# A hybrid decoder step on one core: one loop written out, the first norm reordered, the tail's parts in another order

## The reference

```
merged = sigmoid(ga) * u_a + sigmoid(gb) * u_b ;  mix = merged @ w_o
h = layer_norm(ALPHA * x + mix, ln1_w, ln1_b)
u = h @ w_up ;  g = h @ w_gate
acc = conv_b + sum_i up[:, i:i + t] * conv_w[i]       # up = the two earlier rows, then u
f = (gelu(acc) * g) @ w_down
y = layer_norm(ALPHA * h + f, ln2_w, ln2_b)
```

## Time and profile before

| | us |
|---|---|
| median of 3 runs | 2138.0 (2134.36 to 2139.96) |
| the profiled execution | 2139.22 |
| its span | 2137.5 |
| PE busy | 1989.5 (93%) |
| DVE busy | 1159.1 (54%) |
| ACT busy | 648.8 (30%) |
| POOL busy | 218.8 (10%) |

### The profile page before, as it was taken

The page is one execution under the profiler, slowest core; times in us unless marked ns, Lnnn a source line. Parts: engine busy times, 40 slices in busy tenths (PEclk is TensorE's granted clock), DMA queues, the critical chain, the costliest instruction groups (busy, mean ns, idle before and its releaser), DMA issues.

```text
span 2137.5 us, 39105 instructions
## 1 busy us (share of the span) xinstructions
PE 1989.5 (93%) x14335; PEld 1861.5 (87%) x14335; DVE 1159.1 (54%) x1771; ACT 648.8 (30%) x1179; POOL 218.8 (10%) x253
## 2 busy tenths in 40 slices
PE   7898998899999899989898898799999999999996
PEld 5796896798898798878798897799999999999996
DVE  4554454977867867885424856533322333233348
ACT  4444343134133223213401103434301322132224
POOL 1000000020020020020000101300000000100004
PEclk9999999999999999989999999899999999999999
DMA  4211101787987878886732310111111111111144
GB/s 126 63 32 50 40 21 51 233 311 245 310 281 262 301 264 298 278 308 231 252 94 89 106 49 11 40 49 40 50 49 50 40 48 43 54 42 49 43 142 131
DMA packets 151682, 276.50 MB, mean 129 GB/s; under 512 B 19042, under 2 KB 57951, under 8 KB 151543
## 3 DMA queue, kind: packets, MB, share of 16 engines
q1 hardware_dynamic: 115970, 175.26, 24.4%
q0 software_dynamic: 23232, 82.80, 13.0%
q10 hardware_dynamic: 12368, 16.88, 2.1%
HBM read 247.24 MB, written 27.72 MB: 129 GB/s over the span
## 4 chain that ended last, share of the span: by engine, by line
PE 44%; DVE 5%; DMA 1%; issue 1%; ACT 1%; SPq 0%; DVEq 0%; ACTq 0%
PE bank L121 40%; PE bank L1670 3%; DVE x_lo L1898 1%; DMA gated_raw<-gated_t_scratch 1%; DVE chunk_tmp L1827 1%; DVE chunk_tmp L1829 0%; DVE z L1895 0%; DVE moving_lo L1833 0%; DVE merged_hi L1831 0%; PE banks L1628 0%; DVE w_lo L1968 0%; DMA tail_raw<-in_w_down_dram 0%; DVE y L1944 0%; DMA z<-fox_t_scratch 0%; PE banks L1656 0%
## 5 line engine op out<-in xcount | busy, mean ns | idle before, releaser
L121 PE MATMUL bank<-x_hi,w_hi 128*128 128x344 f32 (+1 forms) x1944 | 641.5, 330 | 44.4 <-DVE x_lo L1898 15.1
L121 PE MATMUL bank<-x_lo,w_hi 128*128 128x344 f32 (+1 forms) x1944 | 631.6, 325 | 0.0
L121 PE MATMUL bank<-x_hi,w_lo 128*128 128x344 f32 (+1 forms) x1944 | 631.3, 325 | 0.0
L121 PEld LDWEIGHTS bank<-x_hi,w_hi 128*128 128x128 f32 (+1 forms) x1944 | 372.4, 192 | 61.6 <-issue 48.6
L121 PEld LDWEIGHTS bank<-x_lo,w_hi 128*128 128x128 f32 (+1 forms) x1944 | 372.5, 192 | 1.6
L121 PEld LDWEIGHTS bank<-x_hi,w_lo 128*128 128x128 f32 (+1 forms) x1944 | 372.1, 191 | 1.7
L97 ACT ACTIVATE w_hi<-w_raw 128x1024 fp32r<-128x1024 f32 (+3 forms) x139 | 142.1, 1022 | 453.7 <-PE bank L121 419.5
L121 PE MATMUL bank<-moving_hi,w_hi 128*128 128x344 f32 x744 | 227.0, 327 | 13.7 <-DVE moving_hi L1806 7.0
L121 PE MATMUL bank<-moving_lo,w_hi 128*128 128x344 f32 x744 | 237.6, 319 | 0.0
L104 DVE TENSOR_TENSOR w_lo<-w_raw,w_hi 128x1024 fp32r<-128x1024 f32 (+3 forms) x139 | 164.4, 1182 | 103.2 <-ACT w_hi L97 101.4
L121 PE MATMUL bank<-moving_hi,w_lo 128*128 128x344 f32 x648 | 208.1, 321 | 0.0
(11 more groups left out here) (275 smaller groups left out, 2781.3 us busy)
## 6 DMA issues: line engine op xcount, KB each, us to landing
cache_keys<-in_cache_k_dram SPq DMA_DIRECT2D x256, 256.0 KB, 4.8
cache_vals<-in_cache_v_dram SPq DMA_DIRECT2D x256, 256.0 KB, 5.1
w_raw<-in_w_in_dram POOLq DMA_DIRECT2D x52, 512.0 KB, 6.3
w_raw<-in_w_up_dram POOLq DMA_DIRECT2D x22, 512.0 KB, 4.5
w_raw<-in_w_gate_dram POOLq DMA_DIRECT2D x22, 512.0 KB, 4.5
tail_raw<-in_w_down_dram SPq DMA_DIRECT2D x22, 448.0 KB, 3.9
gate<-gate_t_scratch SPq DMA_DIRECT2D x15, 516.0 KB, 3.5
w_raw<-in_w_down_dram POOLq DMA_DIRECT2D x10, 448.0 KB, 4.4
```

What stands on the lines that cost most here:

```text
L121: mm = pe.matmul(g.bank[n][0:m, 0:TC], w[slot][:, k, 0:m], x[:, k, chunk(n)], start=(k == 0 and i == 0), stop=(k == kt - 1 and i == 2))
```

## The change

Three places. In `fox`, the loop of two rounds is written out on all five engines, so the waits are against constants and no branch is left.

In the first norm, the remaining order is: DVE splits the first gate job between the first and the second centring; then per chunk DVE only multiplies by rstd (`scale`), ACT applies weight and bias in place (`h_full`) and rounds in a second instruction, and DVE takes the remainder (`h_low`), alternating with the `scale` of the next chunk. PE works on up and gate of the first tile at once, chunk by chunk, slice by slice, the gate in three other banks. POOL takes its share of `acc` later, from the finished h. The first feed-forward tile is written out ahead of the loop on each engine, without the split that was moved.

In the tail, the parts are blocks 5 to 8, 2 to 4, and 0 and 1 (392, 384 and 256 columns), so seven blocks are spread over the tiles and two follow the last one. The second norm's weight and bias are issued behind four of the tail's weight tiles.

```diff
             def _(pe):
-                with pe.Fori(0, NIT) as it:
+                for it in range(NIT):
...
-    THIRD = 3
-    EDGE = (0, 3 * P, 6 * P, T)
-    tail = [(i, i // KD, i % KD) for i in range(NCH * KD)]
-    turned_after = {KD * (t // THIRD + 1) + 1 + 2 * (t % THIRD): t for t in range(2 * THIRD)}
+    PARTS = ((5, 6, 7, 8), (2, 3, 4), (0, 1))
+    SPANS = ((5 * P, T), (2 * P, 5 * P), (0, 2 * P))
+    ROWS = sum(PARTS, ())
+    EARLY = NT - len(PARTS[-1])
+    tail = [(i, i // KD, i % KD) for i in range(len(PARTS) * KD)]
+    part_of = [p for p, rows in enumerate(PARTS) for _ in rows]
+    turned_after = {KD * (part_of[r] + 1) + 1 + 2 * PARTS[part_of[r]].index(ROWS[r]): r for r in range(EARLY)}
...
-                for w, name in enumerate(("ln2_w", "ln2_b")):
-                    sp.dma_start(wide[w][:], a[name].to_broadcast([P, D])).then_inc(ln_land, 16)
                 for i, _, m in tail[RING:]:
+                    if i == RING + LANDS:
+                        for w, name in enumerate(("ln2_w", "ln2_b")):
+                            sp.dma_start(wide[w][:], a[name].to_broadcast([P, D])).then_inc(ln_land, 16)
...
                         up_and_gate(0, f0, ju)
+                        up_and_gate(1, f0, ju)
                         for k in range(NCH):
-                            pool.wait_ge(normed, (k + 1) * KD)
+                            pool.wait_ge(h_full, (k + 1) * KD)
+                            pool.wait_ge(h_lo, (k + 1) * KD)
                             for t in range(KD):
-                                ins = pool.tensor_scalar(acc[:, t, chunk(k)], z[:, t, chunk(k)], ln_cols[:, 1, t:t + 1], ALPHA, ALU.add, ALU.mult)
+                                ins = pool.tensor_scalar(acc[:, t, chunk(k)], z[:, t, chunk(k)], ALPHA, None, ALU.mult)
...
+                for n in range(NCH):
+                    for (j, slot), dst in ((up_job, bank[n]), (gate_job, gate_bank[n])):
+                        pe.wait_ge(g.w_split, RING + j + 1)
+                        pe.wait_ge(g.bank_free[n], ju + 1)
+                        for k in range(KD):
+                            pe.wait_ge(h_lo, n * KD + k + 1)
+                            for q, (w, x) in enumerate(((g.w_hi, g.xh), (g.w_hi, g.xl), (g.w_lo, g.xh))):
+                                mm = pe.matmul(dst[:, 0:TC], w[slot][:, k, :], x[:, k, chunk(n)],
+                                               start=(k == 0 and q == 0), stop=(k == KD - 1 and q == 2))
+                        mm.then_inc(g.mm_chunk, 1)
...
                         act.wait_ge(normed, n * KD + k + 1)
-                        act.activation(g.xh[:, k, chunk(n)], z[:, k, chunk(n)], ACT.Identity, bias=ln_cols[:, 1, k:k + 1]).then_inc(h_hi, 1)
+                        act.activation(z[:, k, chunk(n)], z[:, k, chunk(n)], ACT.Identity, scale=ln_cols[:, 0, k:k + 1], bias=ln_cols[:, 1, k:k + 1]).then_inc(h_full, 1)
+                        act.wait_ge(h_full, n * KD + k + 1)
+                        act.activation(g.xh[:, k, chunk(n)], z[:, k, chunk(n)], ACT.Copy).then_inc(h_hi, 1)
...
                 squares(0)
+                split_hi(g, act, job(JF, JF % 2, 1))
                 squares(1, range(0, 3))
...
+                centre(0)
+                split_lo(g, dve, job(JF, JF % 2, 1))
+                centre(1)
+                centre(2)
...
+                invert(0)
+                for k in range(KD):
+                    scale(0, k)
+                for n in range(NCH):
+                    if n < NCH - 1:
+                        invert(n + 1)
+                    for k in range(KD):
+                        h_low(n, k)
+                        if n < NCH - 1:
+                            scale(n + 1, k)
```

More of the change, by code:

```diff
@@ L424, in _ @@
             def _(pool):
-                with pool.Fori(0, NIT) as it:
+                for it in range(NIT):
                     for u in range(2):
@@ L438, in _ @@
                     sp.dma_start(dst[:], c[src]).then_inc(const_land, 16)
-                with sp.Fori(0, NIT) as it:
+                for it in range(NIT):
                     for u in range(2):
@@ L542, in _ @@
                 act.nop().then_inc(fo_out, 2)
-                with act.Fori(0, NIT) as it:
+                for it in range(NIT):
                     for u in range(2):
@@ L626, in _ @@
                 dve.wait_ge(const_land, 48)
-                with dve.Fori(0, NIT) as it:
+                for it in range(NIT):
                     for u in range(2):
@@ L1674, in _ @@
                         turn_rows(turned_after[i])
-                for t in range(2 * THIRD, NT):
-                    turn_rows(t)
+                for r in range(EARLY, NT):
+                    turn_rows(r)
             @block.scalar
@@ L1732, in _, with tile @@
                 h_high(2)
-                act.wait_ge(h_lo, NCH * KD)
                 act.wait_ge(z_part, 2)
                 for s, (f0, n, ju, jd) in enumerate(sections):
-                    with act.Fori(0, n) as i:
+                    def tile(i, first):
                         f = i + f0
-                        split_hi(g, act, job(i * 2 + ju, ju % 2, 1))
+                        if not first:
+                            split_hi(g, act, job(i * 2 + ju, ju % 2, 1))
                         act.wait_ge(conv, f * 5)
@@ L1760, in _ @@
                         act.activation(cr, bank[3][0:NS + 2, 0:P], ACT.Copy).then_inc(cr_out, 1)
+                    if s == 0:
+                        tile(0, True)
+                    with act.Fori(1 if s == 0 else 0, n) as i:
+                        tile(i, False)
                     def down(it):
@@ L1925, in _ @@
                                           gh[:, ds(i, 1), :].rearrange("p a t -> p (a t)").bitcast(F32), ALU.subtract).then_inc(a_lo, 1)
+                    if s == 0:
+                        tile(0, True)
+                    with dve.Fori(1 if s == 0 else 0, n) as i:
+                        tile(i, False)
                     def down(it):
@@ L1968, in tail_lo @@
                         dve.tensor_tensor(g.w_lo[slot][:, 0:KT, :], tail_raw[(i - RING) % LANDS][:], g.w_hi[slot][:, 0:KT, :].bitcast(F32), ALU.subtract).then_inc(g.w_split, 1)
-                for i, third, m in tail:
+                for i, part, m in tail:
                     tail_lo(i + 1)
-                    lo, hi = EDGE[third], EDGE[third + 1]
+                    lo, hi = SPANS[part]
                     chunk_ready(g, dve, JT + i, NCH - 1)
@@ L1976, in _ @@
                             step(turned_after[i - after])
-                for t in range(2 * THIRD, NT):
-                    measure_rows(t)
-                    scale_rows(t - 1)
-                    invert_rows(t)
+                for r in range(EARLY, NT):
+                    measure_rows(r)
+                    scale_rows(r - 1)
+                    invert_rows(r)
                 scale_rows(NT - 1)
                 dve.wait_ge(y_mul, NT)
-                dve.wait_ge(y_add, QB)
-                dve.tensor_tensor(y[QB][0:NS, :], y[QB][0:NS, :], wide[1][0:NS, :], ALU.add).then_inc(y_add, 1)
+                dve.wait_ge(y_add, NT - 1)
+                dve.tensor_tensor(y[ROWS[-1]][:], y[ROWS[-1]][:], wide[1][:], ALU.add).then_inc(y_add, 1)
 def w_in_tile(a, col, m=P):
```

167 lines of the change are left out of this document (93 added, 74 removed).

## The result

The changed kernel took 2111.6 us (median of 4 runs, 2109.1 to 2115.5) against 2139.0 for the kernel before in the same comparison. The ratio is 0.9878, with a 95% interval of 0.9858 to 0.9897: 26 us less, 22 to 30. Predicted were 2120 us and a range of 2113 to 2127: faster as forecast, but by about half as much again. The profiled execution took 2109.1 us, span 2107.3, granted clock 0.979 (before 0.970).

The account below looks back on a forecast made before the run. PE, busy 93% of the span, was taken as the bound. Terms -7.0 - 5.0 - 4.1 - 2.4 + 0.6 + 2.4 - 2.3 = -17.8 us gave 2121.4 profiled, 2120 as median; 8-in-10 range 2113 to 2127.

Parts of the forecast that it names:

- The loop written out: Attention loop's turn: 4.3 us of PE idle time and 2.7 of low clock go, 7.0 us gained, bounds 3 and 8.
- the low clock behind it: After the loop's turn: some 21 matmuls at 0.13 us more each, 2.7 us, would run at full clock.
- The first norm: First norm reordered: the second feed-forward tile starts at 1369.6 instead of 1374.8, 5 us gained, bounds 0 and 9.
- the 1.2 us for the low clock while slices are fed: First norm, PE: 1.2 us added for matmuls at the lower clock, putting up complete near 1361.5.
- the pairs of 0.98 us: First norm, DVE: each pair takes 0.98 us, so eight take 7.8 us.
- POOL's share: First norm: POOL's late `acc` work ends near 1366, before ACT overwrites that memory near 1368, costing nothing unless 2 us slower.
- ACT doesn't decide: First norm: ACT's two instructions take 1.1 us a slice, last `x_hi` near 1357.5, and don't set the pace.
- The tail's start: Tail's first SP weight tile, issued earlier: 4.1 us of PE idle and 2.4 of low clock gained; wider first part costs 0.6.
- The tail's end: Tail's last tiles lose 2.4 us to one more block; two blocks behind the last tile instead of three gain 2.3.
- Rival 3: Everything lands at its better bound, norm gaining 9 and tail's last part losing 0.9: 2114 us, chance 0.11.
- Rivals 2 and 4: 2: waits go but clock stays low, 2127 us, chance 0.17. 4: loop's idle was the `w_lo` wait, 2126, chance 0.06.
- Rival 5: Slower: the 4.12 us branch is code fetching and returns as stops in straight code; five stops give 2141 us, chance 0.04.

Follow-up runs that it names:

- free: Changed kernel with the hand-over to the second feed-forward tile shortened (weights rounded and split earlier, up's banks freed at ScalarE's copy): ratio 0.9855 to the kernel before.
- one_act: Changed kernel with the first norm's weight multiplied in on VectorE, bias added by each reader, so ScalarE has one instruction a slice: ratio 0.9884 to the kernel before.
- e3_tail: Kernel before with only the tail's edits, the parts' order and the moved fetch of the wide rows: ratio 0.9970.
- wide_only: Kernel before with only the fetch of the second norm's weight and bias moved behind four weight tiles: ratio 0.9971.
- pe_loop: Changed kernel with the attention loop back as a loop on TensorE alone: ratio 0.9924 to the kernel before.
- idle_one: Changed kernel in which TensorE waits once, between second and third pair, until the pair's output is stored: ratio 0.9899 to the kernel before.
- shift_slow: Changed kernel with 149 more instructions (waits already met) at TensorE's start, moving later instruction fetches: ratio 0.9951 to the kernel before.
- after: The changed kernel itself, against the kernel before: 2111.6 us, ratio 0.9878.
- after_again: The changed kernel once more, unaltered: ratio 0.9863 to the kernel before.
- the two pads: Changed kernel with 90 or 45 empty instructions that never got into the program, so repeats of it: ratios 0.9878 and 0.9869 to the kernel before.

## Why the prediction was off

- **The loop written out, 7.0 us predicted, 9.4 and 12.6 timed, 10.6 +- 1.5 by the profiles.** The idle time was right (4.3, measured 4.3), the low clock behind it 1.8 instead of 2.7: the trace before was the worst of eight, 7.5 us for 30 matmuls where the others had 6.4 to 6.9. (The prediction's twelve matmuls in 3 us would be 0.25 us each; the timeline has them 0.29 apart, as it says.) The step that failed is "The stage behind begins at a barrier, so all of it moves forward: 7.0 us", with bounds of 3 and 8. It doesn't only move: the stages from retention to the first centring take 3.4 +- 0.8 us less. TensorE's instructions are fetched at other moments there, which is shown to set two waits, but the two come to 1.6 of the 3.4 us once PE's next waits are counted; for the rest the cause is open. The page of the profile had the queue of these fetches, and I hadn't read it. Of the 17.2 us in the two profiles some 7 are the chance of two executions: centres spread by 2.9 us (one standard deviation) in either kind.
- **The first norm, 5 predicted, 7.2 by the profiles, 9.6 timed (6.2 to 13.3).** Measured from the start of the first centring, predicted and then measured: the moved split's end 8.5 and 9.1, the first reciprocal 14.9 and 15.2, the second chunk's last remainder 42.3 and 41.4, the last `x_hi` 47.5 and 48.1, up complete 51.5 and 49.7, the second tile 58.1 and 56.9, with 1.5 and 1.6 us of low clock behind it. (1351.6 and the 1.1 us for POOL make 1352.7, not the 1352.3 of the prediction, so 42.7.) The terms that failed are the 1.2 us for the low clock while slices are fed and the pairs of 0.98 us: the clock was 1.00 with gaps between every three matmuls (21 in 6 us), and a pair took 0.86. I named `w_lo` as the last wait; its split ended at 1349.17, and PE went on only at 1349.73, behind DVE's first product with the gate. In free both are gone.
- **POOL's share.** Predicted to end 56 us behind the centring and to cost nothing unless 2 us later; it ended at 60.3 and held ACT for 4.2 us, still at no cost to PE. Where DVE met it, remainders took 0.78 us instead of 0.52, five of them in the second chunk: 1.3 us, near the 1.1 that I had and under the 2 estimated from the Trainium skill's lock (SBUF — State Buffer, "Who interferes with whom").
- **ACT doesn't decide** was right, as one_act shows, and for a reason I had not given.
- **The tail's start, 4.1 + 2.4, measured 6.2 and 6.3.** Right. The wider first part costs 0.4 us (30.08 in e3_tail against 29.71 in wide_only), not 0.6.
- **The tail's end, loss 2.4 and gain 2.3.** Between wide_only and e3_tail the last product ends 2.0 us later, the last scaling starts 1.5 earlier (so 3.5 saved behind it, as predicted), and the 512 KB take 0.9 us longer, not 1.2: 0.6 gained with the wider part counted, where the sum had 0.7 lost.
- **The sum**: 10.6 + 7.2 + 6.9 = 24.7 us by profiles against 17.8: 3.6 us of the miss lie in the loop's term, 2.2 in the norm's and 1.1 in the tail's. Rival 3, all at better bounds, was the nearest, and for the wrong reason: no bound held the effect on a later stage. Rivals 2 and 4 are refuted by the clock of 1.00 and by pe_loop. Rival 5 asked the right question, what fetching code costs, but looked for stops in the straight code and not for the fetches among the data.

## What to carry to other kernels

A loop that turns once around a long body, as here, costs TensorE a stop at the turn (4 us), and the written-out code took no more fetches. An edit that makes TensorE's code longer or shorter moves the instruction fetches of all later stages; where such a stage waits for a stream of transfers, read the instruction queue's row, and don't take a difference of a few microseconds there for the edit's own. When a wait has gone, add up the waits behind it too: here the next engine in line took back 3.4 of 5.0 us. Before shortening what feeds an engine, look whether that engine is already at its full rate there, and when a wait has two releasers within a microsecond, take away both.

## What the runs showed of the hardware

- A fetch of 16 KB of instructions takes about 1 us on its queue (0.9 to 1.7 in the trace before). When one began some 7 us ahead of an awaited cache transfer's landing, PE's wait for it was 1 to 2 us longer at two places; 149 and 113 instructions more moved the fetch there and away, and the waits followed.
- An idle time of 3.6 us between full-rate stretches (idle_one) was followed by 1.5 us lost at the low clock, one of 2.5 us at shift_slow's first cache wait by none; gaps of a few tenths between every three matmuls cost none (clock 1.00).
- The same program's first centring came between 1292.9 and 1299.6 us in four profiled executions (after, after_again and the two pads): a part of a profile's difference ahead of a stage is chance, though everything from there to the end repeats to 0.8 us (813.7 to 814.5).
